# Setup of a two-block transformer kernel: w_ada held in the array, another split of the rounding work

## The reference, cut to what matters

```
mod_l = silu(c) @ w_ada + b_ada                    # one condition row, 1024 -> 3072
mod_c = silu(c_ctx) @ w_ada + b_ada                # the same for the context
sh_l, sc_l, gt_l = split(mod_l, 3)
h_lat = rmsnorm(x, norm_g) * (1.0 + sc_l) + sh_l   # 1024 tokens
h_ctx = rmsnorm(ctx, norm_g) * (1.0 + sc_c) + sh_c # 256 tokens
pl = h_lat @ w_in + b_in                           # the projections of attention follow
```

## Time and profile before

| what | value |
|---|---|
| median of 3 runs | 3214.3 us (3212.19 to 3214.42) |
| the profiled execution | 3210.17 us, its span 3208.4 us |
| mean granted TensorE clock in it | 0.974 of full |
| TensorE busy | 3027.8 us, 94% |
| DVE, ACT, POOL busy | 43%, 30%, 32% |
| chain that ended last | TensorE 81%, issue 8%, DVE 6% |

### The profile page before, as it was taken

The page is one execution under the profiler, slowest core; times in us unless marked ns, Lnnn a source line. Parts: engine busy times, 40 slices in busy tenths (PEclk is TensorE's granted clock), DMA queues, the critical chain, the costliest instruction groups (busy, mean ns, idle before and its releaser), DMA issues.

```text
span 3208.4 us, 38389 instructions
## 1 busy us (share of the span) xinstructions
PE 3027.8 (94%) x14387; PEld 2425.3 (76%) x14387; DVE 1367.3 (43%) x2172; ACT 952.0 (30%) x1569; POOL 1015.5 (32%) x801
## 2 busy tenths in 40 slices
PE   7999989999998999999989999978978999999998
PEld 3788768888876877888767888746766888888886
DVE  5344430111011035544387999851275232332325
ACT  3345532122222244231354222242333111111113
POOL 2544322233422345122221333302445332332323
PEclk9999999999999999999999999989988999999999
DMA  5211021111212133111111111102121111111111
GB/s 193 54 37 37 11 85 50 53 46 43 66 51 72 49 92 95 38 27 34 27 47 31 46 49 47 39 1 85 57 66 40 51 47 46 46 52 46 46 52 72
DMA packets 261458, 170.53 MB, mean 53 GB/s; under 512 B 23604, under 2 KB 249452, under 8 KB 260205
## 3 DMA queue, kind: packets, MB, share of 16 engines
q1 hardware_dynamic: 259997, 163.93, 17.1%
q10 hardware_dynamic: 1360, 5.24, 0.4%
HBM read 160.69 MB, written 8.45 MB: 53 GB/s over the span
## 4 chain that ended last, share of the span: by engine, by line
PE 81%; issue 8%; DVE 6%; POOL 2%; ACT 2%; DMA 1%; SPq 0%; POOLq 0%; DVEq 0%; ACTq 0%
PE ps L322 64%; PE ps L3539 2%; PE ps L3538 2%; PE ps L3540 2%; PE ps L2404 2%; DVE score L2985 1%; PE ps L971 1%; PE ps L985 1%; POOL w_lo L306 1%; PE ps L543 1%; DVE ssq L1909 1%; DVE h_lo L1899 1%; PE ps L1490 1%; PE ps L1493 1%; DMA rows<-in_norm_ffn_post 0%
## 5 line engine op out<-in xcount | busy, mean ns | idle before, releaser
L322 PE MATMUL ps<-h_hi,w_hi 128*128 128x512 f32 x2864 | 1142.5, 399 | 53.4 <-POOL w_lo L306 22.7
L322 PE MATMUL ps<-h_lo,w_hi 128*128 128x512 f32 x2864 | 1124.7, 393 | 0.0
L322 PE MATMUL ps<-h_hi,w_lo 128*128 128x512 f32 x2864 | 1123.4, 392 | 0.0
L306 POOL TENSOR_TENSOR w_lo<-raw,w_hi 128x512 fp32r<-128x512 f32 (+2 forms) x556 | 658.9, 1206 | 1394.0 <-ACT w_hi L299 1393.8
L322 PEld LDWEIGHTS ps<-h_hi,w_hi 128*128 128x128 f32 x2864 | 543.7, 190 | 177.1 <-issue 39.8
L322 PEld LDWEIGHTS ps<-h_hi,w_lo 128*128 128x128 f32 x2864 | 543.1, 190 | 116.2
L322 PEld LDWEIGHTS ps<-h_lo,w_hi 128*128 128x128 f32 x2864 | 544.1, 190 | 113.2 <-issue 3.1
L299 ACT ACTIVATE w_hi<-raw 128x512 fp32r<-128x512 f32 (+2 forms) x556 | 288.3, 567 | 891.9 <-PE ps L322 683.3
L3488 DVE TENSOR_TENSOR act<-gate,ps 128x1024 f32<-128x1024 f32 x22 | 26.9, 1221 | 446.1 <-PE ps L322 446.1
L3497 DVE TENSOR_TENSOR acc<-acc,ps 128x1024 f32<-128x1024 f32 x160 | 195.3, 1221 | 28.7 <-PE ps L3540 27.9
L1194 DVE TENSOR_TENSOR part<-sig,ps 128x1024 f32<-128x1024 f32 x40 | 48.6, 1215 | 355.6 <-PE ps L322 274.9
(11 more groups left out here) (423 smaller groups left out, 3589.2 us busy)
## 6 DMA issues: line engine op xcount, KB each, us to landing
raw<-in_w_in SPq DMA_DIRECT2D x88, 512.0 KB, 4.0
raw<-in_w_ffn_gate_up SPq DMA_DIRECT2D x44, 512.0 KB, 3.8
raw<-in_w_out SPq DMA_DIRECT2D x32, 512.0 KB, 3.7
raw<-in_w_gate SPq DMA_DIRECT2D x32, 512.0 KB, 3.6
raw<-in_w_ffn_down SPq DMA_DIRECT2D x22, 512.0 KB, 3.5
w_ada<-in_w_ada SPq DMA_DIRECT2D x8, 1024.0 KB, 7.8
x_tok<-in_x ACTq DMA_DIRECT2D x4, 1024.0 KB, 14.3
residual_gate<-in_w_ada SPq DMA_DIRECT2D x8, 512.0 KB
```

Source lines behind the costliest of these rows:

```text
L306: pool.tensor_tensor(w_lo[:, s, cut], raw[:, s, cut], w_hi[:, s, cut].bitcast(F32), ALU.subtract).then_inc(split.sem, 1)
L322: last = pe.matmul(dst, w[:, chunk[0] % 2, k], x(k), start=(k == ks[0] and n == 0), stop=(k == ks[-1] and n == 2))
```

## The change

Four edits, all in setup and at the start of attention.

- `contract(k)` holds w_ada and moves the conditions: sixteen products a block, each with its own 128x128 block of w_ada loaded and 2 columns moved, accumulating in 32 columns of ps[2]. The result lies across partitions at once; the copy of the two rows and the sixteen transposes are gone.
- ACT makes `cond` ahead of issuing x and the context, not behind.
- Items 0, 2, 4, 6 are cast to hi by DVE, items 1, 3, 5, 7 and both halves of the context by ACT (`high`), between its scalings. All ten lo parts are formed by DVE, none by POOL.
- In attention the product of chunk 1 with the first half of the tokens is put ahead of that of chunk 0 with the context.

```diff
+                ON_DVE = (0, 2, 4, 6)
...
                 def rest_of(engine, n):
                     src, hi, lo = split_of(n)
-                    engine.wait_ge(hi_ready.sem, hi_ready.at(n + 1))
-                    engine.tensor_tensor(lo, src, hi.bitcast(F32), ALU.subtract).then_inc((lo_ready, lo_ready2)[n % 2].sem, 1)
+                    if n in ON_DVE:
+                        engine.wait_ge(hi_ready.sem, hi_ready.at(ON_DVE.index(n) + 1))
+                    else:
+                        engine.wait_ge(hi_ready2.sem, hi_ready2.at(n + 1 - sum(m < n for m in ON_DVE)))
+                    engine.tensor_tensor(lo, src, hi.bitcast(F32), ALU.subtract).then_inc(lo_ready.sem, 1)
...
                     rest_chunk(pool, 0, 0, 4)
-                    for n in range(0, 10, 2):
-                        rest_of(pool, n)
...
                 def _(act):
+                    act.wait_ge(transposed.sem, transposed.at(1))
+                    act.activation(cond[:], ps[0][:, 0:2 * KT].rearrange("p (v t) -> p t v", v=2), ACT.Silu).then_inc(y_ready.sem, 1)
                     x_rows = a["x"][0].rearrange("(t p) d -> p t d", p=P)
                     for n in range(4):
                         act.dma_start(x_tok[:, 2 * n:2 * n + 2], x_rows[:, 2 * n:2 * n + 2]).then_inc(x_parts[n].sem, 16)
                     act.dma_start(c_tok[:], a["ctx"][0].rearrange("(t p) d -> p t d", p=P)).then_inc(x_loaded.sem, 16)
-
-                    act.wait_ge(transposed.sem, transposed.at(1))
-                    act.activation(cond[:], ps[0][:, 0:2 * KT].rearrange("p (v t) -> p t v", v=2), ACT.Silu).then_inc(y_ready.sem, 1)
...
-                    act.wait_ge(aux2.sem, aux2.at(KT))
-                    act.activation(mod_rows[:, 0:D], ps[2][0:2, :], ACT.Copy).then_inc(evicted.sem, 1)
...
+                    def high(n):
+                        src, hi, _ = split_of(n)
+                        act.wait_ge(h_ready.sem, h_ready.at(n + 1 if n < KT else KT + 4 * (n - KT) + 4))
+                        act.activation(hi, src, ACT.Copy).then_inc(hi_ready2.sem, 1)
+
                     for d in range(KT):
                         act.activation(xt[:, d], xt[:, d], ACT.Identity, bias=shift[:, d, 0:1],
                                        scale=scale[:, d, 0:1]).then_inc(h_ready.sem, 1)
+                        if d % 2:
+                            high(d)
...
+                        high(KT + g)
...
                     dve.wait_ge(aux2.sem, aux2.at(KT))
-                    dve.tensor_copy(mod_rows[:, D:2 * D], ps[3][0:2, :]).then_inc(evicted2.sem, 1)
-                    dve.wait_ge(transposed.sem, transposed.at(3))
...
                     for n in range(10):
-                        dve.wait_ge(h_ready.sem, h_ready.at(n + 1 if n < KT else KT + 4 * (n - KT) + 4))
                         src, hi, _ = split_of(n)
-                        dve.tensor_copy(hi, src).then_inc(hi_ready.sem, 1)
-                        if n % 2:
-                            rest_of(dve, n)
+                        if n in ON_DVE:
+                            dve.wait_ge(h_ready.sem, h_ready.at(n + 1))
+                            dve.tensor_copy(hi, src).then_inc(hi_ready.sem, 1)
+                        rest_of(dve, n)
...
                     def contract(k):
                         pe.wait_ge(ada_loaded[k % SLOTS].sem, ada_loaded[k % SLOTS].at(k // SLOTS + 1))
-                        for n in range(4):
-                            last = pe.matmul(ps[2 + n // 2][0:2, n % 2 * HALF:n % 2 * HALF + HALF], cond[:, k],
-                                             w_ada[:, k % SLOTS, n * HALF:n * HALF + HALF], start=(k == 0), stop=(k == KT - 1))
+                        for j in range(2 * KT):
+                            last = pe.matmul(ps[2][:, 2 * j:2 * j + 2], w_ada[:, k % SLOTS, j * P:j * P + P], cond[:, k],
+                                             start=(k == 0 and j == 0), stop=(k == KT - 1 and j == 2 * KT - 1))
                         last.then_inc(aux2.sem, 1)
...
-                    pe.wait_ge(evicted.sem, evicted.at(1))
-                    pe.wait_ge(evicted2.sem, evicted2.at(1))
-                    for j in range(2 * KT):
-                        last = pe.transpose(ps[2][:, 2 * j:2 * j + 2], mod_rows[:, j * P:j * P + P], ident[0:2, 0:2])
-                    last.then_inc(transposed.sem, 1)
...
+                    piece(1, ps[1][:, 0:HALF], tokens_of(0)).then_inc(piece_ready.sem, 1)
                     pe.wait_ge(*h_arrived[8])
                     pe.wait_ge(*h_arrived[9])
                     piece(0, ps[2][:, 0:CTX], tokens_ctx()).then_inc(used.sem, 1)
-                    piece(1, ps[1][:, 0:HALF], tokens_of(0)).then_inc(piece_ready.sem, 1)
```

More of the change, by code:

```diff
@@ L213, in first_then_second_block @@
         hi_ready = signal("hi_ready")
+        hi_ready2 = signal("hi_ready2")
         lo_ready = signal("lo_ready")
@@ L370, in setup @@
                 ctx32 = w_ada[:, 0].rearrange("p (n d t) -> p n d t", n=2, d=4)
-                mod_rows = w_ada[0:2, 1]
                 n_rows = len(ROWS_A) + len(ROWS_B)
+                ON_DVE = (0, 2, 4, 6)
                 PARTS = (TT * P + CTX) // (2 * P)
@@ L587, in _ @@
                     contract(7)
-                    pe.wait_ge(evicted.sem, evicted.at(1))
-                    pe.wait_ge(evicted2.sem, evicted2.at(1))
-                    for j in range(2 * KT):
-                        last = pe.transpose(ps[2][:, 2 * j:2 * j + 2], mod_rows[:, j * P:j * P + P], ident[0:2, 0:2])
-                    last.then_inc(transposed.sem, 1)
-            ended["h_arrived"] = [(half.sem, half.at(n // 2 + 1)) for n in range(10) for half in [(lo_ready, lo_ready2)[n % 2]]]
+            ended["h_arrived"] = [(lo_ready.sem, lo_ready.at(n + 1)) for n in range(10)]
             const_loaded.passed(3)
@@ L605, in setup @@
             for s, n in ((aux, 1), (aux2, KT), (aux3, 1), (aux4, 1), (mod_ready, 2), (stat_ready, PARTS), (norm_ready, PARTS),
-                         (y_ready, 1), (sq_ready, 10), (biased, 1), (exped, 1), (probs, 1), (transposed, 3), (pt_ready, 10), (pt_evicted, TT),
-                         (h_ready, 16), (hi_ready, 10), (lo_ready, 5), (lo_ready2, 5), (evicted, 1), (evicted2, 1)):
+                         (y_ready, 1), (sq_ready, 10), (biased, 1), (exped, 1), (probs, 1), (transposed, 2), (pt_ready, 10), (pt_evicted, TT),
+                         (h_ready, 16), (hi_ready, 4), (hi_ready2, 6), (lo_ready, 10)):
                 s.passed(n)
```

## The result

| | before | after |
|---|---|---|
| median of six runs, us | 3212.37 (3210.68 to 3214.42) | 3227.0 (3223.26 to 3238.2) |
| ratio | | 1.0054 [1.0044, 1.0064] |
| profiled execution, us | 3210.17 | 3227.69, span 3225.9 |
| first scaling on ACT | 57.21 | 72.68 |
| masks issued by SyncE | 81.71 | 93.39 |

The kernel is slower by 0.54%, 14.6 us. The last three rows of the table are start times in the two profiled executions, at the places where I cut the setup in the forecast: the path is 15.5 us late at the first scaling, 11.7 at the masks, 12.1 at the first scores.

The account below looks back on a forecast made before the run. Bound: a chain of waits, nearly all TensorE until 53 us, then DVE, then DMA and POOL. +22.3 - 3.1 + 0.7 = +19.9 on the profiled 3210.2 gives 3230.1, as a median 3234.2 us; range 3226 to 3240.

Parts of the forecast that it names:

- The large term: Setup contractions on TensorE: 32 rows each at the half clock, 6.8 us instead of 3.5 us.
- I take one of five: Full clock returns after one of five transpose groups in setup, winning 3.4 us; bounds none and five.
- My second rival: Setup transposes hold the clock about half the time: five returns to full clock, +6.3, 3220.6 us; chance 0.08.
- Start of the chain: Setup start: cond ahead, x issued near 4.9; first transposes at 15.2 to 18.2, taken 16.5, beside 17.45 before.
- Small steps behind the contractions: Small DVE steps between the contractions and the first token scaling stay, at 1.7 us.
- The split: Token rounding and rests in setup: ACT becomes the bound, 21.4 us instead of 24.5, so -3.1.
- Behind it: After the masks: DMA-POOL chain keeps 19.5 us; TensorE idles some 5 us for weight chunk 1; +0.7 added.
- The tie: Start of attention: TensorE's path of 39 to 42 us beside 40.9 for the DMA chain, from the scaling's start.
- The moved product gains nothing here: Start of attention: chunk 1's product, put ahead of the context, waits for ACT's late rounding and wins no time.
- the sum: Whole kernel: +22.3 to the first scaling, -3.1 for the rests, +0.7 behind them, together +19.9 us.
- the 3227.4 that I gave for three returns: Whole kernel time in us if the full clock returned three times among the setup's transpose groups.

Follow-up runs that it names:

- the control with 64 columns: The changed kernel with 62 columns of zeros moved behind the two conditions in each contraction product: 3207.8 us, ratio 0.999.
- the version that beats both kernels: Changed kernel plus 62 zero columns, x's part 0 ahead of cond, chunk 1 prepared in setup, POOL's chunk 2 rest before its first table: 3197.52 us, ratio 0.9959.

## Why the prediction was right, and where it was not

**The large term had the right mechanism and was too large.** Named: 32 rows a contraction, 0.213 us each at the half clock, the clock down without an idle TensorE. Found: contraction 0 in 32 rows and 6.96 us (0.217 each), and the control with 64 columns at the full clock. The mis-sized step is "I take one of five" returns. It was four in the profiled execution: turn 0 to the last contraction took 52.5 us (19.25 to 71.79) against 61.3. I had argued from a return at 1661.94 behind sixteen transposes and some long products, and priced a return at 3.4 us; both hold. Only the number of returns was wrong, and nothing in the rows spoke for one rather than four: "one" was a guess between none and five. My second rival was closer to that stretch than the forecast.

The Trainium skill (TensorE: Matmul & The Clock Gate, Part 4: PE-mode transpose), by which no transpose would count, is contradicted by the returns behind groups of nothing but transposes, at 54.6 for one. The Trainium skill (the same page, LDWEIGHTS), 0.107 us a load, fits the rows at the full clock (0.110) and misses those at the half (0.207 to 0.217) by a factor of two, as weighed.

**Start of the chain.** x was issued at 3.48, earlier than my 4.9, but its first part took 11.5 us from its issue, more than the 9.2 I had as the upper end: all three blocks of w_ada had been issued ahead of it, and my bound was from w_ada's own block 0. Turn 0 began at 19.25, I had taken 16.5, and my range ended at 18.2: +2.7 missed. Contraction 0 was indeed hidden.

**Small steps behind the contractions:** 0.9 us instead of 1.7. Before, the last of DVE's steps took 0.97 beside POOL's rest of chunk 0; after, POOL is long done and it takes 0.17. First scaling therefore +15.5 instead of +22.3: +2.7 for x, -10.2 for three more returns (3 x 3.4), +0.6 for the transposes (17.7 us for 17.1), +1.1 for contractions at 6.96 rather than 6.8, -0.8 here, which is -6.6 of the -6.8.

**The split:** 20.7 us for 21.4, -3.8 for -3.1, with ACT without a gap and DVE at 1.23 us, as described. The 0.15 us that I gave ACT for waiting on its own result came from no row; the chain of the kernel after has 0.02 there (75.06 to 75.08), which is most of the difference.

**Behind it:** the wait for chunk 1's rest was forecast at 5 us and is 4.50, from 21.8 us behind the first scaling (said: 21.9). The tie was broken by TensorE: 32.6 us from the masks to the first score, 32.2 before, so +0.4 for +0.7. "The moved product gains nothing here" holds; it costs 1.5.

**What the sum left out.** To the first score it gives +19.9 and the trace has +12.1. But the profiled pair is 17.5 us apart at the end. The other 5.4 us come later, in steps of 1 to 2 us, some at changes of the granted clock that fall on other work. In the other profiled executions this later part, taken against the same execution of before, lies between -0.6 and +6.5 us with no order in it: before's own profiled execution was a quick one, 3210.17 beside its median of 3212.37. Whether any of the 5.4 belongs to the change I can't say. Last, I added 4.1 us for the difference between before's median (3214.3) and its profiled execution; with more runs that difference is 2.2, and in the change it is -0.7. So 3234.2 against 3227.0 is: 7.8 too much in the setup, 5.4 too little behind it, and 4.8 too much for the medians. The time lies 1 us inside the lower end of the forecast's own range (3226 to 3240), and it lies there by misses that partly cancel: that part is luck. So is the match with the 3227.4 that I gave for three returns, where the trace has four and an x that is 2.7 us late. Two of the six executions (3223.33, 3223.26) lie below that range.

## What to carry to other kernels

Ask of a product with few moved columns what it does to the clock, not only what its loads cost: here 2 columns behind each 128x128 block halved TensorE's pace while it showed 100% busy, and 62 columns of zeros, which cost nothing beside the load, gave it back. Price each edit of a bundle on the path by itself: three of these four summed to nothing, and the one that shortened its stretch (rests that no longer collide, -3.8 us) was not clear of the noise in the total by itself; the version that beats both kernels has it and moves the waits behind it too. When a wait is taken away, look at the next thing on the same queue before you count the gain.

## What the runs showed of the hardware that I had not expected

- Behind groups of sixteen fp32 transposes, with nothing between the contractions but them, the granted clock goes from 0.50 to 1.00 (four times in the changed kernel, the first of them by the price alone), and under products with 2 moved columns it falls again (54.6 to 58.1); without transposes it stayed at 0.50 for 41 us of unbroken work. The same group does not do it every time (contraction 1: 3.82 and 6.62 us in two kernels equal up to there).
- A 4 KB load of condition rows lands 1.35 us after its issue when no x was issued ahead of it (with 64 columns) and 4.3 us when 1 MB of x was issued 0.9 us earlier on another engine's queue; x, 1 MB, lands 6.2 us after its issue when it is first and 11.5 us when 3 MB of w_ada were issued ahead of it.
